# Triangular inverse of a gated delta rule: 16x16 diagonal blocks by substitution on VectorE, then three doubling levels on 64 columns

## The reference

```python
lower = jnp.where(strict, jnp.einsum('bnhik,bnhjk->bnhij', kb, k) * decay, 0.0)
tri = lower + jnp.eye(CHUNK, dtype=jnp.float32)
rhs = jnp.concatenate([vb, kb * jnp.exp(g)[..., None]], axis=-1)
sol = lax.linalg.triangular_solve(tri, rhs, left_side=True, lower=True)
```

## Time and profile before

| | us |
|---|---|
| median of 3 runs | 1626.65 |
| the runs | 1626.57 to 1631.96 |
| the profiled execution | 1628.99 |
| its span, first to last instruction | 1625.8 |
| heads 0 to 6 of the delta stage | 680 (95 to 775) |
| head 7 | 93 (775 to 868) |
| mean granted clock of TensorE | 0.985 |

### The profile page before, as it was taken

How to read it: one execution, slowest core, us unless ns; L and a number is a source line. 1 busy time by engine, 2 the same in 40 slices (tenths; PEclk the granted TensorE clock), 3 DMA queues, 4 the chain that set the end, 5 groups by cost and what they waited for, 6 DMA issues and landing times.

```text
span 1625.8 us, 21571 instructions
## 1 busy us (share of the span) xinstructions
PE 1523.3 (94%) x8311; PEld 1242.6 (76%) x8311; DVE 792.0 (49%) x1087; ACT 669.8 (41%) x953; POOL 490.7 (30%) x276
## 2 busy tenths in 40 slices
PE   5999999999999999999688988999999999997897
PEld 4778788787878878787566866877878778785686
DVE  6554555545554555455442132555554554556513
ACT  6143432535334253532542143545544554546303
POOL 8434152332614334152421431122121221212020
PEclk9999999999999999999899999999999999999999
DMA  7210000000000010000004411110101010010323
GB/s 219 80 37 17 26 13 26 26 13 26 14 25 25 26 26 13 26 13 13 1 1 130 155 53 38 31 34 27 37 26 39 26 39 26 27 38 0 100 81 117
DMA packets 98929, 68.67 MB, mean 42 GB/s; under 512 B 2401, under 2 KB 93650, under 8 KB 98898
## 3 DMA queue, kind: packets, MB, share of 16 engines
q1 hardware_dynamic: 98898, 68.23, 14.0%
HBM read 55.64 MB, written 12.58 MB: 42 GB/s over the span
## 4 chain that ended last, share of the span: by engine, by line
PE 59%; issue 24%; POOL 6%; DVE 6%; ACT 4%; DMA 1%; POOLq 0%; SPq 0%; DVEq 0%; ACTq 0%
PE psum L336 37%; PE psum L1391 4%; PE psum L1384 4%; PE psum L1467 4%; PE psum L1493 3%; POOL Lb L556 2%; PE psum L1399 2%; PE psum L1480 2%; POOL sumT L539 2%; DVE stick L1175 1%; POOL decT L562 1%; POOL acc L493 1%; DVE inv L1061 1%; ACT u_hi L648 1%; ACT sq L874 1%
## 5 line engine op out<-in xcount | busy, mean ns | idle before, releaser
L336 PE MATMUL psum<-u_hi,w_hi 128*128 128x512 f32 x1296 | 536.7, 414 | 23.9 <-DVE u_lo L895 8.7
L336 PE MATMUL psum<-u_lo,w_hi 128*128 128x512 f32 x1296 | 533.1, 411 | 0.0
L336 PE MATMUL psum<-u_hi,w_lo 128*128 128x512 f32 x1296 | 523.3, 404 | 0.2
L317 POOL TENSOR_TENSOR w_lo<-w_raw,w_hi 128x1024 fp32r<-128x1024 f32 x81 | 218.1, 2692 | 855.9 <-ACT w_hi L312 855.9
L336 PEld LDWEIGHTS psum<-u_hi,w_hi 128*128 128x128 f32 x1296 | 246.1, 190 | 76.8 <-issue 16.0
L336 PEld LDWEIGHTS psum<-u_hi,w_lo 128*128 128x128 f32 x1296 | 246.2, 190 | 48.2 <-issue 6.6
L336 PEld LDWEIGHTS psum<-u_lo,w_hi 128*128 128x128 f32 x1296 | 246.5, 190 | 46.1 <-issue 6.7
L556 POOL TENSOR_TENSOR Lb<-dec,level 128x512 f32<-128x512 f32 x112 | 145.8, 1322 | 125.7 <-PE psum L1384 111.0
L312 ACT ACTIVATE w_hi<-w_raw 128x1024 fp32r<-128x1024 f32 x81 | 85.3, 1053 | 172.6 <-DVE xT L1134 113.6
L1068 DVE TENSOR_TENSOR invT<-invT,psum 128x512 f32<-128x512 f32 x96 | 66.0, 688 | 111.4 <-PE psum L1391 111.4
L829 ACT ACTIVATE soft<-psum 128x1024 f32<-128x1024 f32 (+3 forms) x64 | 41.8, 653 | 161.9 <-DVE psum L1163 161.4
(11 more groups left out here) (172 smaller groups left out, 2020.6 us busy)
## 6 DMA issues: line engine op xcount, KB each, us to landing
w_raw<-in_a_w_in SPq DMA_DIRECT2D x33, 512.0 KB, 4.1
w_raw<-in_b_w_in SPq DMA_DIRECT2D x32, 512.0 KB, 4.0
resid<-xT SPq DMA_DIRECT2D x16, 512.0 KB, 3.5
res_in<-resid SPq DMA_DIRECT2D x16, 512.0 KB, 4.5
o_all<-in_x SPq DMA_DIRECT2D x8, 512.0 KB, 7.3
w_raw<-in_a_w_out SPq DMA_DIRECT2D x8, 512.0 KB, 3.7
w_raw<-in_b_w_out SPq DMA_DIRECT2D x8, 512.0 KB, 3.7
out<-fin_o SPq DMA_DIRECT2D x8, 512.0 KB, 2.6
```

What stands on the lines that cost most here:

```text
L317: G.tensor_tensor(w_lo[:, b % 2], w_raw[:, b % 2], w_hi[:, b % 2].bitcast(F32), ALU.subtract).then_inc(lo_done, 1)
L336: mm = PE.matmul(psum[:, half], (w_hi, w_hi, w_lo)[part][:, b % 2, k], (u_hi, u_lo, u_hi)[part][:, k, half * HALF:(half + 1) * HALF], star ...
```

## The change

Levels 0 to 3 of the inverse (block sizes 1 to 8) are replaced by a substitution on VectorE that inverts the 16 x 16 diagonal blocks; three doubling levels stay (sizes 16, 32 and 64).

The substitution works on all 8 chunks and 8 blocks at once. Partition p holds row p of L. `small_L` gathers the 16 columns of the own diagonal block (one reduction over `Lb`, 1024 elements for each partition). For row r of the blocks, `stream_shuffle` hands row r of each block to all 16 partitions of that block (`row_L`), a product with the columns found so far goes into `terms`, and a reduction over it with the unit term gives column r of `small_T`. Fifteen rows, three VectorE instructions each, with semaphores between those that depend on each other. Two more products spread `small_T` to the block diagonal of `invT`; TensorE transposes invT, and ScalarE evicts to `inv`, so the roles of inv and invT at the start are swapped.

In a level the matmuls take only those 64 of 128 columns of invT that the level changes (`second`), so X, Xs and the subtraction have half the width. The weights (Lb, inv) stay 128 x 128.

The fills are placed anew: 42 instead of 12 between the token transposes and the start transposes; three in most gaps of the inversion; the recurrence has 2, 3 and 3 instead of 3, 4 and 3 in its middle steps. AT_T0 is 98, the inversion ends at 125, the recurrence at 191. VectorE does two taps behind each of the three levels instead of one behind each of six, and ScalarE in the last head two conversions. GpSimd makes the masks of level 1 as soon as small_L is there. The hardware loops over heads, on all engines and in both stages, become Python loops, so the code is written out for each head. `terms` lies in the memory of sumT.

```diff
-LEVELS = 7
+SMALL = 16
+BLOCKS = P // SMALL
+FIRST_LEVEL = 4
+LEVELS = 4
+SIDE = P // 2
...
-PREP_GAPS = (30, 8, 8, 10, 12)
-INV_GAPS = (5, 2, 2) + (2, 2, 2) * 4 + (2, 4)
-REC_GAPS = (4, 4, 3) + (3, 4, 3) * 5 + (3, 4, 6) + (3, 4, 2)
+PREP_GAPS = (30, 8, 8, 10, 42)
+INV_GAPS = (5, 3, 3) + (3, 3, 3) + (3, 4)
+REC_GAPS = (4, 3, 2) + (2, 3, 3) * 5 + (2, 3, 5) + (2, 3, 2)
...
-        TAP_INV = {l: (l - 1,) for l in range(1, LEVELS)}
+        TAP_INV = {l: (2 * l - 2, 2 * l - 1) for l in range(1, LEVELS)}
...
+        def second(t, l):
+
+            return t.rearrange("p (a b c) -> p a b c", b=2, c=1 << (l + FIRST_LEVEL - 1))[:, :, 1, :]
+
+        def packed(n):
+            return psum[:, n, 0:4 * SIDE].rearrange("p (i c) -> p i c", i=4)
...
-                if n == 0 and (not isinstance(h, int) or h > 0):
-                    args_ready.wait(pool, h - 1, 2)
+                if n == 0 and h > 0:
+                    small_done.wait(pool, h - 1, SMALL - 1)
...
                     if l == 0:
                         gram_done.wait(pool, h, 4 if g else 2)
+                    elif l == 1:
+                        small_in.wait(pool, h, 2)
                     else:
-                        inv_mm[g].wait(pool, h, 1 if l == 1 else 3 * (l - 1) - 1)
-                        if l == 1:
-                            t0_done[g].wait(pool, h, 1)
+                        inv_mm[g].wait(pool, h, 3 * (l - 1) - 1)
...
-                    fill.to(AT_T0 if l < 3 else AT_INV[3 * l - 7])
+                    fill.to(AT_TOK if l == 1 else AT_T0 if l == 2 else AT_INV[3 * l - 7])
...
-                    A.activation(half_of(invT, g), bank(2 + 2 * g), ACT.Copy).then_inc(inv_ev[g].handle, 1)
+                    A.activation(inv[:, g], bank(2 + 2 * g), ACT.Copy).then_inc(inv_ev[g].handle, 1)
...
-                        A.activation(Xs[:, g], bank(2 + 2 * g), ACT.Copy).then_inc(inv_ev[g].handle, 1)
+                        A.activation(Xs[:, g, :, 0:SIDE], packed(2 + 2 * g), ACT.Copy).then_inc(inv_ev[g].handle, 1)
...
+                args_ready.wait(dve, h, 2)
+                V.tensor_copy(terms[:, :, ::SMALL + 1], own_col[:, :].unsqueeze(1).broadcast_to((P, NC, SMALL))
+                              ).then_inc(small_in.handle, 1)
                 for g in range(2):
                     lb_done[g].wait(dve, h, 1)
-                    V.scalar_tensor_tensor(out=inv[:, g], in0=Lb[:, g], scalar=-1.0,
...
+                V.tensor_reduce(small_L[:, :, :], flat4(Lb).rearrange("p (n b c) -> p n c b", n=NC, b=BLOCKS),
+                                axis=mybir.AxisListType.X, op=ALU.add, negate=True).then_inc(small_in.handle, 1)
+
+                def row(r):
+                    small_in.wait(dve, h, 2)
+                    V.stream_shuffle(row_L[:, r % 2, :, 0:r], small_L[:, :, 0:r],
+                                     [SMALL * (i // SMALL) + r for i in range(32)]).then_inc(row_done.handle, 1)
+
+                row(1)
+                for r in range(1, SMALL):
+                    of_row = terms[:, :, SMALL * r:SMALL * r + r + 1]
+                    row_done.wait(dve, h, r)
+                    if r > 1:
+                        small_done.wait(dve, h, r - 1)
+                    V.tensor_tensor(of_row[:, :, 0:r], row_L[:, r % 2, :, 0:r], small_T[:, :, 0:r], ALU.mult
+                                    ).then_inc(terms_done.handle, 1)
+                    if r + 1 < SMALL:
+                        row(r + 1)
+                    terms_done.wait(dve, h, r)
+                    V.tensor_reduce(small_T[:, :, r:r + 1], of_row, axis=mybir.AxisListType.X, op=ALU.add
+                                    ).then_inc(small_done.handle, 1)
+                    if r % 5 == 0:
+                        fill.to(AT_TOK + (AT_T0 - AT_TOK) * r // SMALL)
+                small_done.wait(dve, h, SMALL - 1)
+                for g in range(2):
+                    V.tensor_tensor(half_of(invT, g).rearrange("p n (b r) -> p n b r", b=BLOCKS),
+                                    small_T[:, 4 * g:4 * g + 4, :].unsqueeze(2).broadcast_to((P, 4, BLOCKS, SMALL)),
+                                    own_block[:, :].unsqueeze(1).unsqueeze(3).broadcast_to((P, 4, BLOCKS, SMALL)),
+                                    ALU.mult).then_inc(t0_done[g].handle, 1)
...
-                        V.tensor_tensor(half_of(invT, g), half_of(invT, g), bank(3 + 2 * g), ALU.subtract
-                                        ).then_inc(inv_up[g].handle, 1)
+                        size = 1 << (l + FIRST_LEVEL - 1)
+                        changed = flat(half_of(invT, g)).rearrange("p (x b c) -> p x b c", b=2, c=size)[:, :, 1, :]
+                        V.tensor_tensor(changed, changed,
+                                        psum[:, 3 + 2 * g, 0:4 * SIDE].rearrange("p (x c) -> p x c", c=size),
+                                        ALU.subtract).then_inc(inv_up[g].handle, 1)
...
-            with dve.Fori(0, H - 1) as h:
+            for h in range(H - 1):
...
-                            mm = PE.matmul(psum[:, 2 + 2 * g, i * P:(i + 1) * P], Lb[:, g, i],
-                                           invT[:, 4 * g + i, :], start=True, stop=True)
+                            mm = PE.matmul(psum[:, 2 + 2 * g, i * SIDE:(i + 1) * SIDE], Lb[:, g, i],
+                                           second(invT[:, 4 * g + i, :], l), start=True, stop=True)
...
-                            mm = PE.matmul(psum[:, 3 + 2 * g, i * P:(i + 1) * P], inv[:, g, i], Xs[:, g, i],
-                                           start=True, stop=True)
+                            mm = PE.matmul(psum[:, 3 + 2 * g, i * SIDE:(i + 1) * SIDE], inv[:, g, i],
+                                           Xs[:, g, i, 0:SIDE], start=True, stop=True)
```

More of the change, by code:

```diff
@@ L149, in build @@
         level = sd("level", [P, LEVELS, P])
+        own_block = sd("own_block", [P, BLOCKS])
+        own_col = sd("own_col", [P, SMALL])
+        small_L = sd("small_L", [P, NC, SMALL])
+        small_T = sd("small_T", [P, NC, SMALL])
         after_f = v_new[:, :]
@@ L428, in _ @@
             load_w(sp, 0, 3, wa_v[:, :, 3 * D:3 * D + P])
-            with sp.Fori(1, H) as h:
+            for h in range(1, H):
                 for b in range(4):
@@ L524, in _ @@
             G.memset(raw[:, :, 0:3], 0.0).then_inc(consts, 1)
-            n = levels(2, LEVELS, n + 1)
+            n = levels(1, LEVELS, n + 1)
+            G.memset(own_block[:, :], 1.0).then_inc(consts, 1)
+            blocks_of(own_block[:, :], SMALL, False, n + 1)
+            n += 3
             assert n == CONSTS_A
@@ L614, in _ @@
             serve_b(0)
-            with pool.Fori(1, H) as h:
+            for h in range(1, H):
                 serve_b(h)
@@ L783, in _ @@
             act.sem_inc(oln_done.handle, 2)
-            with act.Fori(0, H - 1) as h:
+            for h in range(H - 1):
                 head(h, True)
@@ L1442, in head @@
                 fill.to(QUAD)
-            with pe.Fori(0, H - 1) as h:
+            for h in range(H - 1):
                 head(h, True)
```

51 lines of the change are left out of this document (35 added, 16 removed).

## The result

| | before | after |
|---|---|---|
| median of 6 runs each, us | 1630.75 | 1638.2 |
| lowest to highest | 1626.57 to 1631.96 | 1636.99 to 1638.71 |
| the profiled execution | 1628.99 | 1637.95 |
| its span | 1625.8 | 1636.2 |
| mean granted clock | 0.985 | 0.938 |

The ratio is 1.0055 (95% interval 1.0043 to 1.0067): slower, clear of no change, by about the half per cent that a measurement of this kernel can tell. I had forecast 1612, a change of -14.6 us from the 1626.65 of three runs; with three more runs of before its median is 1630.75. By the medians the change is +7.45 us, between the two profiled executions +9.0.

What follows compares the result with a forecast made beforehand. TensorE (busy 94% of the span) bounds seven heads, a chain of latencies the eighth. Seven heads give -12.2 us, the last -2.4: -14.6, so 1614.4 from the profiled 1628.99, or 1612 against the 1626.65 median; range 1572 to 1645.

Steps and rivals of the forecast that it cites:

- dear-chain rival: Fifteen substitution rows before the start transposes: at 0.84 us a row, +27.6 us, so 1640; chance 0.33.
- so 1.85 us are lost behind it: Heads with fill, behind TensorE's 9.6 us stall: 3.7 us at half clock, costing 1.85 us a head.
- The last head: Head without fill: +12.5 us up to the start transposes, -16.8 for three levels, smaller terms; net -2.4 us.
- signs of being wrong: Wait under 5 us, row over 0.73, narrow matmuls under 0.08 apart, or the attention stage changing its length.
- Levels removed: Inverse in heads with fill: each level removed frees 4.58 us of TensorE, three free 13.7 us a head.
- loops: Hardware loops written out as straight code on all engines: no effect, zero us.
- The waits at the recurrence: Recurrence in heads with fill: 0.8 us before it, 1.7 us from the third fill missing at n = 1 to 7.
- The wait: TensorE before the start transposes in heads with fill: waits 9.6 us for the start matrix where it waited 1.1.
- A row: Substitution on VectorE: product, shuffle and sum take 0.61 us a row, 9.15 for fifteen; bounds 0.35 and 0.90.
- The lock of POOL: Row products waiting for the port GpSimd holds during masks and a weight split: 4.0 us, bounds 0 and 5.5.
- Gathering small_L: VectorE before the rows: reading 1024 elements takes 1.22 us, as the 1024-element product.
- The 64 columns: Level matmuls, 96 a head: no gain from narrowing; bounds -5.1 and +1.2 us a head.

Runs made afterwards that it cites:

- experiment 2: Kernel after, with unread matmuls filling TensorE's stops (25 before product 96, 9 before the start transposes, 68 in the last head): 1604.6 us, ratio 0.9854.
- experiment 11: Kernel after, with its levels on all 128 columns and unread matmuls filling TensorE's stops: 1602.7 us, ratio 0.9843.
- experiment 12: Kernel before, with 18 unread matmuls in front of the start-matrix transposes in its last head: 1628.5 us, ratio 1.0001.
- experiment 5: Kernel after, with level-1 masks put in another buffer before the rows and the second weight split behind the level-2 masks: 1613.3 us, ratio 0.9904.
- experiment 7: experiment 6 with 57 fills instead of 42 before the start transposes and fewer in the levels: 1567.7 us, ratio 0.9626.
- experiment 9: experiment 7 with 50 unread matmuls in front of the start-matrix transposes in the last head: 1566.3 us, ratio 0.9621.
- experiment 6: experiment 5 plus masks before the first split, unit terms early, v_beta behind the spreading, the fill's eviction at row 4: median 1623.6 us, ratio 0.9959.
- experiment 8: Kernel after, with its three levels on all 128 columns again, evictions and subtraction too: 1624.5 us, ratio 0.9975.

## Why the prediction was wrong

The forecast was 1612, the result 1638.2, inside the range of 1572 to 1645 but on the other side of no change, which I had given 0.24. The number of the dear-chain rival (1640) is near, by luck: its mechanism, a row of over 0.73 us, is not what happened. Against the forecast the profiled span came out 25 us longer: 13.9 in the seven heads, 6.5 in the last head, 3.8 in the rest and 0.9 in the prologue.

**The step that failed** is the term "so 1.85 us are lost behind it", the half clock behind a stall. I read from rows 13 that PE, after 6 us idle, ran 3.7 us at 0.51, and made the stall of 9.6 us do the same. In four heads the number held, 1.6 to 1.9 us, but not what stood behind it: the stretch at half clock was 8.5 us and not 3.7, and it cost so little because PE was busy in only 5.4 of it, part of that in front of the wait for the start matrix, where nothing was lost. That the number held was luck. In three it cost about 7, since the clock stayed at 0.50 for 17 us in place of 8.5. Three times 5.2 above my term is 15.6 us, and the seven heads came out 682.2 - (680.5 - 12.2) = 13.9 above the forecast. I took one stretch of one head as the law, and gave it no upper bound, though other terms had theirs. Kept busy, the heads behind the first took 93.1 on average; my sum without this term is 95.1 - 1.85 = 93.25.

**The last head** was to be 2.4 us shorter and is 4.1 longer. Up to the start transposes it lost 13.3 us (12.5 forecast): PE waits 16.9 us where it waited 3.8. From there on I forecast a gain of 14.9, and it gained 70.2 - 61.0 = 9.2. The window of PE behind the wait:

```profile
814.00:844.00 30.00, 27.85 (x124) 0.50 0.00 1
```

Thirty us at half clock behind the wait, for which I had no term at all. In experiment 2, where 14 us of that stretch are at 0.99 and 16 at 0.50, the same part takes 56.4, a gain of 13.8; in experiment 11, with the wide levels, the 16 us are at 0.89, and it takes 54.3, a gain of 15.9. The 14.9 of the forecast lies between.

**The rest of the program** was to stay as it was, and grew by 3.8 us, clock again (experiment 12). That was one of the signs of being wrong that I had named. The prologue, also put at nothing, grew by 0.9; I did not look for the cause.

**Right, or off in size only:**
- Levels removed, fills, recurrence, loops: the sum of 93.25 for a head at full clock against 93.1 measured; written-out loops ratio 1.0002. (The "six fills" of a level in my sum are six products, two in each of three gaps.) The waits at the recurrence are 0.7 us in its first step, where I had put 0.8, and 0.3 behind it, where I had put 1.7.
- The wait: 8.9 to 9.6 us idle (9.52 in the head shown) against 9.6. I had it as one stop at the start matrix; it is two, in the head shown 6.57 at product 96 and 2.95. I overlooked that the fill can't pass product 96 without an eviction that stands behind row 10.
- A row: 0.63 us without the lock (experiment 5) against 0.61. The lock of POOL: 0.95 + 0.75 + 2.0 = 3.7 us on the products of rows 1, 2 and 7, against 4.0. Gathering small_L: 1.92 against 1.22; I had priced a reduction over strided elements by a product of as many.
- The 64 columns: nothing on PE (0.106 us each against 0.107). I misread the rule that spoke for a gain. The Trainium skill (TensorE: Matmul & The Clock Gate, section Back-to-back issue gap) gives its about 60 cycles for 1 to 64 columns as an isolated gap, and says beside it that in a stream of weight loads and matmuls both set the spacing. This trace, where each matmul has its own 128 columns of weights, agrees with that sentence, and its pitch with the estimate by the section LDWEIGHTS of the same page, 107 ns. The narrowing is worth 0.3 us a head, on ACT and DVE (experiment 11).
- The dear chain: the shuffle's selection is indeed loaded by a fourth instruction, as the Trainium skill says (Vector Engine (DVE) Microarchitecture Reference, section 3.8), and it takes 0.01 us here.

**What stays open:** why the same stop is followed by 8.5 us at half clock in one head and by 17 in the next, or by none. Experiments 7 and 9 show that it isn't the length of the last wait, and the waits of the kernel after that it isn't the length of the whole stop. Between heads of the same code and the same stop what differs is the time at which the stop falls; whether that decides, no run tests.

## What to carry to other kernels

A stop of TensorE costs more than its length: behind it everything on the engine may run at half speed, for a time that one trace doesn't bound. So a change that trades steady TensorE work for a serial chain on another engine should be costed with the dearest stretch at half clock, and built with enough independent TensorE work moved in front of the chain's end (experiment 7: the same work in another order, 70 us less than the kernel after). Before reading anything into a difference of one per cent, lay the granted clock of the same stretch of both kernels side by side, also where the code is the same, and fill the stops with unread matmuls to take the clock out of the comparison.

## What the runs showed that I had not expected

- Two lengths of the stretch at half clock, behind the same stop in the same code: 8.5 and 17 us. The clock split one kernel's executions in groups some 20 us apart (experiment 6), and made a kernel with more work 14 us faster (experiment 8).
- The same matmuls take longer in one kernel than in another. The rest of the program, 3466 PE instructions in all fourteen profiled executions, took 757.5 to 761.4 us, with PE idle for 43.4 to 44.3 in each.
- A stop of 1.7 to 1.9 us can be enough, or not. In experiment 7 the timeline of PE at two start transposes, and then the windows behind each, read:

```profile
221.41 1.17 PE L1451 MATMUL psum<-ident,invT 128*128 128x128 f32 x8 [1.93 <-DVE invT L1129]
311.79 1.17 PE L1451 MATMUL psum<-ident,invT 128*128 128x128 f32 x8 [1.67 <-DVE invT L1129]
```
```profile
222.80:233.00 10.20, 10.20 (x47) 0.52 0.18 47
...
312.50:324.00 11.50, 11.43 (x92) 1.00 0.17 47
```

- In the last head of experiment 9, 31 us at 0.51 began right behind a wait of 2.6 us in front of which PE had been busy at 1.00 for 14 us.
- VectorE's small shuffles cost 0.18 to 0.29 us, a selection load 0.01, and a reduction of 1024 strided elements 1.92 us where a product of 1024 takes 1.22.
